# Clearing and filling the decoder's masked operands behind level 64 of the triangular solve

## The reference

```python
a_mat = jnp.eye(c, dtype=F32) + m
sol = lax.linalg.triangular_solve(a_mat, rhs, left_side=True, lower=True, unit_diagonal=True)
w_blk, u_blk = sol[..., :dk], sol[..., dk:]
...
q_dec = qb * jnp.exp(gc)[..., None]
...
def step(s, xs):
    w_c, u_c, q_c, a_c, k_c, d_c = xs
    v_new = u_c - jnp.einsum('bhcd,bhde->bhce', w_c, s)
    o_c = jnp.einsum('bhcd,bhde->bhce', q_c, s) + jnp.einsum('bhcs,bhse->bhce', a_c, v_new)
    s = s * d_c[..., None, None] + jnp.einsum('bhcd,bhce->bhde', k_c, v_new)
    return s, o_c
```

## Time and profile before

| | |
|---|---|
| median of 3 runs | 1349.88 us (1349.31 to 1349.89) |
| span of the profiled execution | 1347.1 us; no device time of that execution is given beside it |
| PE busy | 1296.2 us, 96% |
| PE weight loads busy | 1091.4 us, 81% |
| DVE busy | 857.1 us, 64% |
| ACT busy | 582.9 us, 43% |
| POOL busy | 54.3 us, 4% |
| granted TensorE clock | 0.8 in three of 40 slices, 0.9 or more in the others |

### The profile page before, as it was taken

How to read it: one execution, slowest core, us unless ns; L and a number is a source line. 1 busy time by engine, 2 the same in 40 slices (tenths; PEclk the granted TensorE clock), 3 DMA queues, 4 the chain that set the end, 5 groups by cost and what they waited for, 6 DMA issues and landing times. The chain is left out here.

```text
span 1347.1 us, 24949 instructions
## 1 busy us (share of the span) xinstructions
PE 1296.2 (96%) x10594; PEld 1091.4 (81%) x10594; DVE 857.1 (64%) x1346; ACT 582.9 (43%) x751; POOL 54.3 (4%) x104
## 2 busy tenths in 40 slices
PE   7999899999999999989999999999999999999996
PEld 3667797799999967669877999999867787876673
DVE  2678558555444457865767544644555769999896
ACT  1352334353342325334424433333335556777762
POOL 7000030000000000002100000000000000000000
PEclk8999999999999999989999999999999999999998
DMA  9666645955544553556442835634656779999990
GB/s 318 230 229 233 234 150 188 327 157 157 166 163 155 174 162 102 212 164 220 134 127 70 259 102 161 215 122 150 207 187 206 223 245 296 343 339 352 342 340 36
DMA packets 190038, 276.07 MB, mean 205 GB/s; under 512 B 7845, under 2 KB 136127, under 8 KB 184808
## 3 DMA queue, kind: packets, MB, share of 16 engines
q1 hardware_dynamic: 177856, 263.62, 58.7%
q10 hardware_dynamic: 12072, 10.86, 2.8%
HBM read 268.16 MB, written 6.30 MB: 204 GB/s over the span
## 5 line engine op out<-in xcount | busy, mean ns | idle before, releaser
L823 DVE TENSOR_TENSOR lo_raw<-raw,hi 128x2048 fp32r<-128x2048 f32 (+2 forms) x112 | 229.4, 2056 | 99.7 <-ACT hi L1933 61.0
L1933 ACT ACTIVATE hi<-raw 128x2048 fp32r<-128x2048 f32 (+2 forms) x112 | 193.6, 1728 | 113.6 <-PE bank L1095 78.2
L1063 PE MATMUL bank<-UH,hi 128*128 128x288 f32 x704 | 209.3, 297 | 0.3 <-DVE lo L2384 0.3
L1065 PE MATMUL bank<-UL,hi 128*128 128x288 f32 x704 | 207.0, 294 | 0.0
L2384 DVE TENSOR_TENSOR lo<-raw,hi 128x2048 fp32r<-128x2048 f32 (+1 forms) x42 | 95.8, 2282 | 85.6 <-ACT hi L2169 48.5
L1064 PE MATMUL bank<-UH,lo_raw 128*128 128x288 f32 x496 | 147.2, 297 | 0.0
L1063 PEld LDWEIGHTS bank<-UH,hi 128*128 128x128 f32 x704 | 132.0, 188 | 0.9 <-DVE lo L2384 0.6
L1065 PEld LDWEIGHTS bank<-UL,hi 128*128 128x128 f32 x704 | 132.5, 188 | 0.0
L1064 PE MATMUL bank<-UH,lo 128*128 128x288 f32 x432 | 127.4, 295 | 0.0
L1093 PE MATMUL bank<-hi,UGH 128*128 128x512 f32 (+9 forms) x288 | 111.7, 388 | 0.0
L1095 PE MATMUL bank<-hi,UGL 128*128 128x512 f32 (+9 forms) x288 | 107.9, 375 | 0.0
(11 more groups left out here) (497 smaller groups left out, 2690.4 us busy)
## 6 DMA issues: line engine op xcount, KB each, us to landing
raw<-in_w_ada_dram SPq DMA_DIRECT2D x48, 1024.0 KB, 7.5
raw<-in_w_in_dram SPq DMA_DIRECT2D x28, 1024.0 KB, 8.3
raw<-in_w_exp_gate_dram SPq DMA_DIRECT2D x26, 1024.0 KB, 5.9
raw<-in_w_exp_up_dram SPq DMA_DIRECT2D x26, 1024.0 KB, 7.8
raw<-in_w_exp_down_dram SPq DMA_DIRECT2D x16, 1024.0 KB, 5.2
raw<-in_w_exp_down_dram SPq DMA_DIRECT2D x16, 768.0 KB, 4.6
raw<-in_w_ff_gate_dram SPq DMA_DIRECT2D x11, 1024.0 KB, 5.5
raw<-in_w_ff_up_dram SPq DMA_DIRECT2D x11, 1024.0 KB, 5.4
```

The costliest lines, as they stand in the source:

```text
L823: dve.tensor_tensor(lo_x[g % XRAW][:, 0:XG[g][2] * XG[g][3]], x_raw(g), hi_x[g % XSPLIT][:, 0:XG[g][2] * XG[g][3]].bitcast(F32), ALU.subtr ...
L1063: pe.matmul(out, wh, xh, start=start, stop=False)
L1065: return pe.matmul(out, wh, xl, start=False, stop=stop)
L1933: act.activation(hi_x[q][:, 0:XG[g][2] * XG[g][3]], x_raw(g), ACT.Copy).then_inc(S("x_hi_made"), 1)
```

## The change

The last three instructions of `qd` on DVE, the two clears and the fill of `QM`, become a step of their own, `qm`, which stands behind `Y` of level 64. `QD` stays where it was. No other engine has work in `qm`, and nothing is added or taken away. It happens once in each layer.

```diff
@@ steps_of
         solve('X', 64)
         filler()
         solve('Y', 64)
+        one('qm')
         filler()
         one('tokv')
@@ block.vector, step
                 elif k == 'qd':
                     dve.wait_ge(S("decays"), 4 * l + 3)
                     dve.tensor_tensor(QD[:, :, :], QKV[:, 0:H, P:NP_], EG[:, 0:H, :], ALU.mult)
+                elif k == 'qm':
                     dve.memset(WM[:, :, :, :], 0.0).then_inc(S("wm_cleared"), 1)
                     then(dve.memset(QM[:, :, :, :], 0.0))
                     dve.tensor_tensor(QM[:, :, :, 0:NT], QKV[:, 0:H, NP_:N].rearrange("p h (q t) -> p h q t", q=NSEQ),
```

## The result

The changed kernel takes 1352.57 us (median of 22 runs, 1348.05 to 1355.5), the kernel before, run beside it, 1349.89 us (22 runs, 1345.22 to 1352.38). The ratio is 1.0018, 95% interval 1.001 to 1.0027: some 2.4 us slower, where 1349.0 us was forecast, and beyond the 1351.3 us to which the range reached. The loss is small, and single executions of either kernel lie 7 us and more apart, so a profile and a median must not be mixed up here.

What follows compares the result with a forecast made beforehand. PE was taken as the bound, busy 1296.2 of 1347.1 us. Terms -0.90 + 0 + 0 + 0 gave a span of 1346.2 us, and with 2.8 us added a median of 1349.0 us; range 1347.0 to 1351.3 us.

Steps and rivals of the forecast that it cites:

- the gain at level 8: Layer 0, level 8: DVE's `mod` ends 0.90 us earlier, cutting PE's wait from 1.43 to 0.53 us; gain 0.90 us.
- Layer 1: Level 8 of layer 1: DVE's gain ends in PE's 2.75 us stop in level 16's products; gain 0.
- Behind level 64: The moved 2.66 us of DVE work is covered in both layers, with no new PE wait; cost 0, twice.
- Whether it is kept: Layer 0, level 16's second products: PE's 1.47 us stop for instructions only moves earlier, keeping 0.90 us; chance 0.45.
- the stop swallowing the gain: Rival, layer 0: PE stands 2.37 us instead of 1.47 and restarts at 143.12 as before; 1349.9 us, chance 0.30.
- a low-clock stretch more: Rival, layer 0: the clock stays low until tile (7,1), which pays 2.1 us, net +1.2; 1351.1 us, chance 0.10.
- The step from the span to the median: Whole kernel: the profiled span is 2.8 us under the median, so 1346.2 us of span becomes 1349.0 us.
- the prediction's two cases: Layer 0's stop: the packet request leaves 0.90 us sooner with PE, or bulk loads hold the packet and the gain is gone.

Runs made afterwards that it cites:

- new order: Kernels without the two clears and the fill on DVE at level 8 of layer 0; seven profiles, mean 20.81 us from level 8's products to level 32.
- old order: Kernels with the two clears and the fill still at level 8 of layer 0; six profiles, mean 19.84 us from level 8's products to level 32.
- the pair of profiles: The first profiles of the changed kernel and the kernel before, from the main measurement; the changed kernel's span is 3.7 us longer.
- Both places: The changed kernel with the two clears and the fill once more at the old place, in both layers: 1351.07 us, 0.9998.
- the closest pair: Profiles of the unchanged repeats of the changed kernel (1349.83 us, 0.9992) and the kernel before (1350.4 us, 0.9988), both from the third follow-up job.
- the first job: The main measurement, ahead of the follow-ups: changed kernel 1352.57 us against 1349.89 us of the kernel before, ratio 1.0018.
- jobs 1 to 4: The four follow-up jobs, each with the kernel before beside it and the changed kernel repeated: 1.0013, 1.001, 0.9992 and 0.9998.
- the four repeats: The changed kernel measured again without edits, once in each follow-up job: 1351.4, 1351.81, 1349.83 and 1351.02 us.
- Layer 0 alone: The kernel before with the clears and the fill moved in layer 0 only: 1350.76 us, 1.0003.
- the variant on GpSimd: The changed kernel with the clears and the fill taken off DVE and done by GpSimd once `UL` is made: 1350.2 us, 0.9997.
- the filled kernel of job 3: The changed kernel with 13 unread products on PE at layer 0's stop and 30 in layer 1: 1352.99 us, 1.002.
- job 4: Fourth follow-up: 7 and 12 unread products in the changed kernel (1352.29 us, 1.0005) or kernel before (1349.38 us, 0.9986), plus unchanged repeats (1351.02, 1351.09 us).
- job 1: First follow-up: changed kernel again (1351.4 us), kernel before again (1350.84), change in layer 0 only (1350.76) and layer 1 only (1351.56).
- the filling of the right size: Seven unread products on PE at layer 0's stop and twelve in layer 1, added to the kernel before: 1349.38 us, 0.9986.
- one of twice the length: Filling with 13 unread products in layer 0 and 30 in layer 1: 1352.99 us, 1.002 in the changed kernel; 1354.26 us, 1.0019 in the kernel before.

## Why the prediction was wrong

*What bounds the kernel, and the gain at level 8: right.* All seven profiles of the new order have PE's wait for `mod` at 0.52 or 0.53 us, and the stage ahead of it is 0.90 us shorter (in each of them 16.35 to 16.37 us between the same two matmuls, against 17.26 or 17.27 in four of the old order). Level 8's subtraction by DVE starts 1.23 us behind PE's products (131.54 - 130.31), as was taken over from level 16.

*Layer 1: right.* The stop there takes DVE's gain; the kernel with the change in layer 1 alone can't be told from no change, and in the pair of profiles the difference stays between 1.8 and 1.9 us from level 32 of layer 0 on. The stop is not the same: 3.10 us in the changed kernel, 2.55 to 3.10 in the 13 profiles.

*Behind level 64: right.* No wait of PE, the low part of (9,1) ends at 166.68 + 1.22 = 167.90 us, which is 165.2 without the 2.7 us of lag from ahead of the change (165.0 was forecast). Both places, where the trio costs DVE twice, is no slower than before.

*Whether it is kept: this step failed.* The prediction read the stop of 1.47 us as something that PE carries with it: "it leaves 0.90 us sooner, and the stop only moves". It named the other case, the stop swallowing the gain, at 0.30, and a low-clock stretch more at 0.10, as two separate rivals. They are one chain. When PE reaches level 16's second products earlier, its packet comes only partly earlier: 0.47 us in the mean for 0.90, and some 0.4 us for 1.03 in the closest pair. So the stop gets longer, 1.59 us in the mean of the new order against 0.96 in the old (with the profile that has none). And at this place the granted clock went with the stop: 1.2 GHz at the end of each of the nine stops of 1.20 us or more, and 2.4 GHz behind the three of 0.65 to 0.93. The prediction had one profile of the kernel before, which happened to be one of the two of six with a long stop and the low clock, and took it as the kernel's constant state. The sum had -0.90 us in layer 0 and put the stop and the clock at 0. What the profiles give for the same stage is -0.46 us at the restart and +1.36 us behind it, +0.9 us for the twelve with a stop and +1.0 us for all thirteen. That is near the +1.2 of the rival "a low-clock stretch more", but by another place: not tile (7,1) pays it, but the rest of level 16 and the transposes behind it, and it came with the stop, not with when the tile begins.

*The step from the span to the median: a small error.* The prediction added 2.8 us to the profiled span. In every execution on record the device time is 1.7 to 1.8 us above its span (1352.56 against 1350.8 us in the changed kernel's profile). So the profile of before was probably of an execution near 1348.9 us, a fast one, and no picture of the median; the forecast of a difference doesn't change by it.

The Trainium skill ("Runtime: NRT & Kernel Launch", section "Instruction fetch mechanics") has the sequencer fetch the next block while it executes the current one. The packets agree: in the closest pair one passes while PE is busy, some 2.4 us ahead of the restart. That PE stands still for want of the next block is inferred from this distance, which is 2.3 to 2.7 us in all twelve profiles; no view names the wait.

*What stays open.* The times of whole executions don't confirm a loss of this size. The five ratios of the changed kernel have a mean of 1.0006 (+0.8 us), more than half of it from the first job; the three of the kernel before against itself have 0.9994 (-0.9 us), where 1 is right, so a mean of a few ratios can be off by as much. In jobs 1 to 4 the mean of 48 executions of the changed kernel is 1351.3 us and that of 168 of the kernel before 1351.1: +0.3 us with a standard error of 0.4. Their mean granted clocks are 0.9869 and 0.9873. That speaks against the forecast gain, and leaves open whether there is a loss. In the profiles the low-clock stretches of the whole execution add up to 38 us in the mean of the new order and 41 us in the old, so what the stage loses doesn't show in the sum. The +2.4 us of the first job, which put the time beyond the range, is more than the stage explains, and the rest of it was not found; the four repeats lie between -1.1 and +1.8 us. Layer 0 alone, with the longest stop, measured 1.0003, and the variant on GpSimd 0.9997. With the stop filled, none of four profiles has a low clock behind it in layer 0, so there the low clock hung on the stop. A length from which it falls does not follow: in level 8, ahead of the change's effect, it fell behind stops of 0.48 (the filled kernel of job 3), 1.03 and 1.03 us (job 4) and not behind one of 0.62 (job 1). Why a packet comes sooner or later was not settled either: the prediction's two cases, a request bound to PE and loads that stand in its way, are both untested. The low-clock stretches at 118 and 668 us have a cause that no run here touched.

## What to carry to other kernels

An engine that outruns its instruction queue has a place where it stands still for nothing that the program names; ask of every gain ahead of it whether it arrives behind it. Such a pause is no constant of the kernel: take several profiles of the kernel before, and look at whether the granted clock falls behind the pause, since a pause that is a little longer can cost more than the gain that lengthened it. Filling such a pause with throwaway products kept the clock up in four profiles, but did not clearly make the kernel faster: the filling of the right size in the kernel before gave 0.9986 (0.9972 to 1.0), and one of twice the length cost 0.2%. Do not call a difference of 0.1% of such a kernel real before the kernel before, measured against itself, comes out closer than that.

## What the runs showed of the hardware that was not expected

- The stop for instructions in level 16's second products varied from nothing to 2.02 us between executions; in all twelve profiles that have it, one 16 KB packet of the instruction queue starts 2.3 to 2.7 us ahead of the restart.
- The low-clock stretch at the end of such a stop lasted 3.4 us in six of the nine cases, 6.8 us in two and 13.7 us in one, the last 6 us of which PE was busy without a pause. The stage behind the stop took 1.4 to 1.5 us longer with 3.4 us of it, and 2.6 us longer with more.
- A 128x128 float32 product whose result nobody reads took 0.24 to 0.26 us (13 of them, 26 records, in 3.17 us; 7, 14 records, in 1.83 us).
- Twelve products put ahead of the stop in layer 1 replaced one stop of 2.75 us by two, of 0.67 and 0.74 us with the old order, the second one in other products. With those products in place no low-clock stretch began in layer 1 near 587 us.
